# A one-core decoder layer: where a tenth product, the silu of c and the states' step sizes stand

## What is computed

```python
mod = silu(c) @ w_ada + b_ada                       # c: one row of 1024
shift, scale, gate = split(mod, 3)
h = rmsnorm(x, norm_pre) * (1 + scale) + shift
u_pool, z_pool, u_ssm, z_ssm, g_pool, g_ssm = split(h @ w_in, 6)
y_pool = causal_pool_mixer(u_pool, pool_w, pool_scale) * silu(z_pool)
dt = exp(log_dt); abar = exp(lam * dt)              # lam complex, 64 groups x 64 states
y_ssm = s5_mixer(u_ssm, abar, ...) * silu(z_ssm)    # scan over the tokens, gelu, sigmoid GLU
merged = sigmoid(g_pool) * (y_pool @ w_branch_pool) + sigmoid(g_ssm) * (y_ssm @ w_branch_ssm)
out = x + gate * rmsnorm(merged @ w_out, norm_post)
```

## Time and profile before

| what | value |
|---|---|
| median of three runs | 934.12 us (933.94 to 934.65) |
| the profiled execution | 933.93 us |
| its span, from the first to the last instruction | 932.1 us |
| PE busy | 909.8 us (98%) |
| DVE busy | 726.2 us (78%) |
| ACT busy | 389.0 us (42%) |
| POOL busy | 45.3 us (5%) |
| mean rate of the transfers | 182 GB/s |

### The profile page before, as it was taken

The page is one execution under the profiler, slowest core; times in us unless marked ns, Lnnn a source line. Parts: engine busy times, 40 slices in busy tenths (PEclk is TensorE's granted clock), DMA queues, the critical chain, the costliest instruction groups (busy, mean ns, idle before and its releaser), DMA issues.

```text
span 932.1 us, 11810 instructions
## 1 busy us (share of the span) xinstructions
PE 909.8 (98%) x4312; PEld 763.3 (82%) x4312; DVE 726.2 (78%) x1057; ACT 389.0 (42%) x534; POOL 45.3 (5%) x82
## 2 busy tenths in 40 slices
PE   3999999999999999999999999999999999999996
PEld 3888888888888888888888888888888888887885
DVE  5988899887777888546789589948468786679977
ACT  5841353343444444344544353623144460136443
POOL 0019900000000000000000000000000000000000
PEclk9999999999999999999999999999999999999999
DMA  9843265545455364437799676476355268454233
GB/s 351 313 142 106 118 228 184 163 159 158 161 195 184 143 225 175 180 75 199 191 265 244 132 198 156 132 247 231 114 226 203 95 225 320 182 198 154 76 106 135
DMA packets 97449, 169.85 MB, mean 182 GB/s; under 512 B 38768, under 2 KB 55280, under 8 KB 97392
## 3 DMA queue, kind: packets, MB, share of 16 engines
q1 hardware_dynamic: 87600, 164.55, 54.1%
q10 hardware_dynamic: 9792, 4.56, 1.9%
HBM read 121.88 MB, written 47.19 MB: 181 GB/s over the span
## 4 chain that ended last, share of the span: by engine, by line
PE 96%; DVE 1%; ACT 1%; DMA 1%; issue 0%; ACTq 0%; DVEq 0%
PE ps L2537 41%; PE ps L2691 32%; PE psb L2691 13%; PE ps L2762 2%; PE psb L2742 2%; PE psb L2751 2%; PE psa L2730 2%; PE psa L2617 1%; PE psa L2537 1%; DMA par_are<-in_a_re 1%; PE psb L2617 0%; PE psb L2567 0%; ACT gt L1196 0%; DVE mod_out L1747 0%; PE psa L2567 0%
## 5 line engine op out<-in xcount | busy, mean ns | idle before, releaser
L2537 PE MATMUL ps<-bop,w_hi 128*128 128x512 f32 x864 | 232.2, 391 | 0.8 <-DVE bop L1789 0.8
L2537 PEld LDWEIGHTS ps<-bop,w_hi 128*128 128x128 f32 x864 | 161.2, 188 | 33.7 <-issue 0.9
L2537 PE MATMUL ps<-bop,w_lo 128*128 128x512 f32 x432 | 133.0, 389 | 0.0
L2537 PEld LDWEIGHTS ps<-bop,w_lo 128*128 128x128 f32 x432 | 81.1, 188 | 17.0
L2691 PE MATMUL ps<-bop,r_hi 128*128 128x512 f32 x272 | 83.7, 389 | 0.0
L1743 DVE TENSOR_TENSOR w_lo<-raw,w_hi 128x1024 fp32r<-128x1024 f32 x35 | 43.4, 1239 | 37.8 <-ACT w_hi L1182 37.5
L1182 ACT ACTIVATE w_hi<-raw 128x1024 fp32r<-128x1024 f32 x35 | 36.9, 1053 | 76.6 <-PE ps L2537 68.4
L2691 PEld LDWEIGHTS ps<-bop,r_hi 128*128 128x128 f32 x272 | 51.1, 188 | 10.6
L2691 PE MATMUL ps<-t_hi,r_hi 128*128 128x512 f32 x140 | 55.1, 393 | 0.0
L2691 PE MATMUL ps<-t_hi,r_lo 128*128 128x512 f32 x140 | 54.6, 390 | 0.0
L2691 PE MATMUL ps<-t_lo,r_hi 128*128 128x512 f32 x140 | 54.5, 389 | 0.0
(11 more groups left out here) (464 smaller groups left out, 1889.0 us busy)
## 6 DMA issues: line engine op xcount, KB each, us to landing
raw<-in_wstream SPq DMA_DIRECT2D x36, 512.0 KB, 5.4
pair_raw<-in_wstream SPq DMA_DIRECT2D x30, 512.0 KB, 4.2
ada<-in_w_ada SPq DMA_DIRECT2D x16, 512.0 KB, 11.3
x_tok<-in_x SPq DMA_DIRECT2D x8, 512.0 KB, 7.0
gs_d<-gt SPq DMA_DIRECT2D x8, 512.0 KB, 4.9
win_d<-win_new SPq DMA_DIRECT2D x8, 512.0 KB, 2.7
wout_d<-wout_new SPq DMA_DIRECT2D x8, 512.0 KB, 3.8
wout<-wout_d SPq DMA_DIRECT2D x8, 512.0 KB, 4.8
```

Of the source, the lines that this page charges most:

```text
L2537: last = mm(ps[slot(u)][:, f * HALF:f * HALF + HALF], a[:, k, :], b(k, f), start=k == order[0] and q == 0, stop=k == order[-1] and q == 2)
```

## The change

Five things change. (a) The product zs7 leaves FILL, where it stood in round 0 between part_b and the next u_pool product, and becomes the tenth entry of FIRST, behind zs0; its load, its two splits, its evacuation and its store move along, and the pairs swap the two sets of buffers (side, SLOT). (b) c is loaded as one row by ScalarE's queue, ahead of the par loads, instead of as 128 equal rows behind x by SP's; ScalarE takes the silu of that row first of all, TensorE multiplies it by a column of ones into psa, and VectorE copies the 128 rows back. ScalarE's function table for the square root is now loaded between its second and its third square. (c) plain_angles moves on VectorE from the front of the program to behind the last low part of h. (d) In the k-steps of gs0 to gs2 TensorE takes high h with both parts of the weights first and waits for low h only ahead of the third part. (e) In the rounds SP starts the load of the next state weights (win) ahead of the tables of round 1.

```diff
-FIRST = [("gs", n) for n in range(KT)] + [("zs", 0)]
+FIRST = [("gs", n) for n in range(KT)] + [("zs", 0), ("zs", 7)]
-FILL = {0: [("zs", 7)], 4: [("zp", 6)], 7: [("zp", 7)]}
+FILL = {4: [("zp", 6)], 7: [("zp", 7)]}
 def side(j):
-    return (j + (j < NP)) % 2
+    return j % 2
...
 # SP
-            sp.dma_start(silu_row[:, :], c_d).then_inc(c_in, 16)
...
             store_gs(6)
+            load_w(9)
...
+            sp.wait_ge(job_out[slot(("zs", 7))], evicted(("zs", 7)))
+            sp.dma_start(zs_d[7], gt[1][:, :]).then_inc(zs_stored[1], 16)
...
             load_u(1)
-            load_tables(1)
             for m in range(KT):
                 sp.wait_ge(x_done, m + 1)
                 if not last:
                     load_win(m + 1)
+                if m == 0:
+                    load_tables(1)
...
 # ScalarE
+            act.dma_start(silu_row[0:1, :], c_d[0:1, :]).then_inc(c_in, 16)
             act.dma_start(par["ldt"], log_dt_d).then_inc(par_in, 16)
...
+            act.wait_ge(c_in, 16)
+            fn(silu_row[0:1, :], silu_row[0:1, :], ACT.Silu).then_inc(silu_ready, 1)
-            act.wait_ge(c_in, 16)
-            fn(silu_row[:, :], silu_row[:, :], ACT.Silu).then_inc(silu_ready, 1)
...
             pair_high(0, P3)
+            act.wait_ge(gs_stored[1], 16 * 4)
+            evac(("zs", 7), gt[1][:, :], ACT.Silu)
             pair_high(0, P4)
...
 # VectorE
-            dve.wait_ge(par_in, 16 * 3)
-            plain_angles(steps)
+            nc.vector.memset(ones[0:1, :], 1.0).then_inc(ones_made, 1)
+            dve.wait_ge(silu_spread, 1)
+            nc.vector.tensor_copy(silu_row[:, :], psa[:, :]).then_inc(silu_copied, 1)
...
             split_h(KT - 1)
+            dve.wait_ge(par_in, 16 * 3)
+            plain_angles(steps)
             reduced_angles(steps)
             sine(steps)
             split_lo(3)
...
             t_sums(3)
+            split_lo(9)
...
 # TensorE
-                pe.wait_ge(h_done, k + 1)
-                last = k_step(u, k, *h)
+                pe.wait_ge(h_hi_done, k + 1)
+                for q, (a, part) in enumerate(((hi, h[0]), (lo, h[0]), (hi, h[1]))):
+                    if q == 2:
+                        pe.wait_ge(h_done, k + 1)
...
+            pe.wait_ge(ones_made, 1)
+            pe.wait_ge(silu_ready, 1)
+            for f in range(2):
+                last = mm(psa[:, f * HALF:f * HALF + HALF], ones[0:1, :], silu_row[0:1, f * HALF:f * HALF + HALF],
+                          start=True, stop=True)
+            last.then_inc(silu_spread, 1)
```

More of the change, by code:

```diff
@@ L410, in build @@
         vta = ssm("vta", [P, GB, CH, SG])
-        zp_t = [t[:, :] for t in (gt[1], rt[1], gt[0], rt[0])]
+        zp_t = [t[:, :] for t in (gt[0], rt[0], gt[1], rt[1])]
         zp_t += [t[:, :, :].rearrange("p g c -> p (g c)") for t in (cos_pa, sin_pa)]
         zp_t += [vta[:, :, :, :].rearrange("p g t h -> p (g t h)"), pu[:, :, :].rearrange("p t c -> p (t c)")[:, 0:SEQ]]
-        zs_last = zp_t[6]
         pfix = ssm("pfix", [P, CH, 2])
@@ L432, in build @@
         silu_row = at("silu_row", [P, D], cur[0])
+        ones = at("ones", [P, P], w_lo_at)
         y_tmp = at("y_tmp", [P, SEQ], cur[0])
@@ L496, in build @@
         c_in, silu_ready, mod_ready = sem("c_in"), sem("silu_ready"), sem("mod_ready")
+        ones_made, silu_spread, silu_copied = sem("ones_made"), sem("silu_spread"), sem("silu_copied")
         mod_acc_done = sem("mod_acc_done")
@@ L532, in build @@
         gs_stored = two("gs_stored")
-        zs_stored = sem("zs_stored")
+        zs_stored = two("zs_stored")
         y_loaded = [sem(f"y_loaded{w}") for w in range(4)]
@@ L1058, in _ @@
             sp.wait_ge(in_lo_done, KT)
-            sp.wait_ge(zs_stored, 32)
+            for s in range(2):
+                sp.wait_ge(zs_stored[s], 16)
             sp.wait_ge(sq_ready, KT)
@@ L1192, in _ @@
                 for t in tiles:
+                    if t == 3:
+                        fn(stat[:, 5, 0:1], cols[:, 0:1], ACT.Sqrt, scale=0.0)
                     act.wait_ge(tile_in[t], 16)
@@ L1298, in pair_high @@
                 elif o >= 4:
-                    act.wait_ge(mm_done, JOB[FIRST[-1 if o < 6 else -2]] + 1)
+                    act.wait_ge(mm_done, JOB[FIRST[-2 if o < 6 else -1]] + 1)
                 u = pair_weights(j)
@@ L1326, in copy_p1 @@
                     act.wait_ge(pair_stored[j % 2], 32 * (j // 2))
[L1327 to L1330, removed]
+                if j < 2:
+                    act.wait_ge(zs_stored[j], 16)
                 act.wait_ge(st_done, S_POS[j, P1] + 1)
@@ L1503, in _ @@
                 for u in FILL.get(m, ()):
[L1504 to L1507, removed]
+                    dst = zp_t[u[1]]
+                    if u == ("zp", 7):
                         act.wait_ge(pooled, KT)
@@ L1789, in split_h @@
                 tt(hb(1, k), halves(h_full[k][:, :]), hb(0, k).bitcast(F32), ALU.subtract).then_inc(h_done, 1)
-            dve.wait_ge(silu_ready, 1)
+            dve.wait_ge(silu_copied, 1)
             for k in range(KT):
@@ L1950, in pair_slot @@
                 elif o >= 4:
-                    dve.wait_ge(mm_done, JOB[FIRST[-1 if o < 6 else -2]] + 1)
+                    dve.wait_ge(mm_done, JOB[FIRST[-2 if o < 6 else -1]] + 1)
             def sum1(j):
@@ L2580, in step @@
                         pe.wait_ge(xt_taken, 4)
-                pe.wait_ge(h_done, k + 1)
-                last = k_step(u, k, *h)
+                pe.wait_ge(h_hi_done, k + 1)
+                hi, lo = (wx_hi, wx_lo) if n == 2 else (w_hi[n % 2], w_lo[n % 2])
+                for q, (a, part) in enumerate(((hi, h[0]), (lo, h[0]), (hi, h[1]))):
+                    if q == 2:
+                        pe.wait_ge(h_done, k + 1)
+                    for f in range(2):
+                        last = mm(ps[slot(u)][:, f * HALF:f * HALF + HALF], a[:, k, :], part(k, f),
+                                  start=k == 0 and q == 0, stop=k == KT - 1 and q == 2)
                 if k == KT - 1:
                     last.then_inc(mm_done, 1)
+            pe.wait_ge(ones_made, 1)
+            pe.wait_ge(silu_ready, 1)
+            for f in range(2):
+                last = mm(psa[:, f * HALF:f * HALF + HALF], ones[0:1, :], silu_row[0:1, f * HALF:f * HALF + HALF],
+                          start=True, stop=True)
+            last.then_inc(silu_spread, 1)
             for tiles in (range(0, 4), range(4, CH)):
                 for k in XT_ORDER[:4]:
+                    if k == 3 and 0 in tiles:
+                        pe.wait_ge(silu_copied, 1)
                     transposed(k, tiles)
@@ L2624, in half_product @@
                 if i == P1:
-                    if j == 0:
+                    if j == 1:
                         pe.wait_ge(job_out[0], SLOT[:len(FIRST)].count(0))
@@ L2653, in half_product @@
                     else:
-                        pe.wait_ge(job_out[j], SLOT[:len(FIRST)].count(j))
+                        pe.wait_ge(job_out[1 - j], SLOT[:len(FIRST)].count(1 - j))
                 elif i == P7:
@@ L2711, in _ @@
             begin(turn0)
-            pe.wait_ge(c21_done, NP - 1)
+            pe.wait_ge(c11_done, NP)
             pe.wait_ge(c12_done, NP - 1)
@@ L2786, in _ @@
                 if m == 0:
-                    pe.wait_ge(c11_done, NP)
+                    pe.wait_ge(c21_done, NP)
                     pe.wait_ge(c12_done, NP)
```

6 lines of the change are left out of this document (1 added, 5 removed).

## The result

The changed kernel takes 938.55 us (five runs, 937.37 to 939.15) against 934.17 (933.94 to 934.70): a ratio of 1.0044, with an interval of 1.0033 to 1.0056. It is slower by 4.4 us. The profiled execution took 937.37, the shortest of the five, with a span of 935.8 us against 932.1, so 3.7 of the 4.4 us can be followed in it.

What follows compares the result with a forecast made beforehand. TensorE, gapless from 26 us on, was taken to bound the kernel: 933.93 + 1.3 (gs3) + 1.2 (states) = 936.4, plus 0.19 for the median, 936.7. Own range 936.0 to 937.5, wide range 935.0 to 938.5.

Steps and rivals of the forecast that it cites:

- rival 3: Before gs3: TensorE's pace falls behind the new wait of 2.6 us, costing up to 1.9 us more, 938.6; chance 0.10.
- The start: Front of the kernel: first sum with w_ada starts at 18.4 instead of 19.71, a gain of 1.3 us.
- plain_angles behind h: Before gs3: 4.47 us more on VectorE, TensorE waits 2.6 us, gs3 begins at 65.7, 1.3 us later than before.
- The clock: Behind the wait before gs3: slower matmuls cost up to 1.9 us; kept out of the sum, as rival 3.
- Low weights behind gs3: gs4 to gs7: low weights come in longer stretches of products, 10.9 us each; coefficients are needed by nothing of FIRST.
- The tenth product: End of FIRST: zs7's low weights there at about 128.3, hidden by a margin of 2.9 us; cost nothing.
- Round 0: Round 0 without zs7: one product of cover fewer, TensorE waits 1.2 us for sq; no second round waits.
- Rival 1: Angles hidden, gs3 starts 1.3 us sooner: 934.0 with the states' wait, 932.8 without; chance 0.10.

Runs made afterwards that it cites:

- filled_wait: The changed kernel with twelve more matmuls of 512 columns, which nothing reads, between gs2 and gs3; 936.50 us.
- product_only: The kernel before with only the tenth product and the load of win ahead of the tables, start as before; 936.12 us.
- front_nine: The changed kernel without the tenth product, plain_angles back at VectorE's front, in its idle time ahead of the copy of the silu; 932.99 us.
- angles_only: The kernel before with plain_angles alone moved behind the last low part of h; 941.07 us.
- product_tables_first: product_only with the tables of round 1 ahead of win again, so the tenth product alone; 936.44 us.
- low_twice: low_first with the low weights of gs7 moved too, ahead of the last coefficients on VectorE; 936.75 us.
- low_first: The changed kernel with the low weights of gs3 ahead of reduced_angles and sine on VectorE instead of behind them; 936.73 us.
- start_only: The changed kernel with zs7 back in round 0 and the tables ahead of win: row of c, later plain_angles and order of parts alone; 936.79 us.
- rotate_first: The changed kernel with VectorE's low weights of round 0 moved from ahead of the rotation to behind it; 938.87 us.

## Why the prediction came out as it did

The direction was right and the size too small: a rise of 2.6 us to 936.7 was forecast, and 4.4 to 938.55 measured. The forecast's own range (936.0 to 937.5) was missed; the wide one reached to 938.5, 0.05 under the median, only because it took in most of rival 3, whose price led up to 938.6.

- **The start**: right. Sums at 18.34 (18.4 forecast), the copy of the silu done at 10.17 (10 allowed, for a sum of 8.7), and x's last tile set the second diagonals, as argued.
- **plain_angles behind h**: right. Low weights at 65.53 (65.6), gs3 at 65.58 (65.7), a wait of 2.8 (2.6).
- **The clock**: this step failed. The forecast took the wait at its length, and put its consequence into a rival with a chance of 0.10. filled_wait showed that it belongs to the sum: 1.6 to 1.7 us in the traces, 2.0 in the medians. The argument against it, that a wait of 0.8 us at 26 us had cost no pace, compared a wait a third as long. That 936.7 + 1.7 = 938.4 meets the median within 0.2 is in part luck: the profiled execution has all three terms and took 937.37, and the 1.2 us from there to the median are in no sum.
- **Low weights behind gs3**: the sentence that the coefficients are needed by nothing of FIRST is wrong. The low weights of gs7 and zs7 stand behind them on VectorE. It did no harm to the number, since TensorE was late itself, and it is where both repairs that were tried lost their gain.
- **The tenth product**: nothing in the changed kernel, as forecast, because of that same delay.
- **Round 0**: the wait for sq was sized rightly (1.05 against 1.2). The taps of the next round, 0.6 us in product_only, were missed: SP's queue takes them up only behind sq and the tables, and the round had lost its 10.9 us of slack. That product is not the only way to this wait: front_nine, with zs7 in its old place, met it in round 3.
- **Rival 1**, that the start carries through, needed the angles hidden. Where they lie in a real gap (front_nine) gs3 does start 1.49 us sooner, and the median is 932.99, where the rival had said 932.8 for a kernel without the states' wait; the profiled execution lost the gain again to the taps.

Open is why four of the five runs took longer than the profiled one, by 0.5 to 1.8 us. The two groups of angles_only show a mean granted clock of 0.997 (937.7 and 937.9) and of 0.995 to 0.996 (941.0 to 942.1), and in the longest run of product_tables_first a transfer was late. Which of the two it was in the changed kernel no trace shows.

## What to carry to other kernels

An engine below full use can still be a second full line in one stretch: before work is moved onto it, add up its instructions between the points where the bounding engine needs it, and look for a place where it is truly idle instead. A wait of a few us on TensorE should be priced with the pace behind it, not by its length alone. When one wait is cured, the next one in the same line has to be priced too, since the first was hiding it.

## What was not expected of the hardware

TensorE's clock did not fall behind every wait. Behind waits of 1.8 us (low_twice), 2.1 (low_first) and 2.4 (angles_only at gs3) the pace stayed; behind 2.8 (the changed kernel and start_only), 3.1 (product_tables_first) and 3.4 (angles_only at the first pair) it halved. rotate_first, with 2.9 at gs3, fell too. Each is one execution. In the last of the three lengths above seven matmuls came at 0.43 us each:

```profile
141.00:144.00 3.00, 3.00 (x7) 0.50 0.00 0
```

The first eight transposes come 0.23 us apart in every kernel, half the pace of the 0.11 later on, while the granted clock reads 1.00, so there the spacing tells more than the column. And log dt, a small load, landed 2.0 us behind its issue as the first of ScalarE's queue, but 4.3 us behind it in the changed kernel (4.0 in start_only, 4.2 in front_nine) as the second, half a microsecond later, when the loads of x had begun. Which of the three does it no run tells apart.
